# 66 more one-pass products behind the last tile of a two-block transformer kernel, most with interleaved moving columns

## The reference, cut to what matters

```
merged = sum over three branches of sigmoid(G_b) * (branch_b @ w_branch_b)   # 256 x 1024
out    = x + merged @ w_out_2                                                # 256 x 1024
```

## Time and profile before

| | us |
|---|---|
| median of two runs | 974.49 |
| the two runs | 974.24, 974.74 |
| span of the profiled execution, first to last instruction | 970.7 |
| run median less that span | 3.8 |
| TensorE busy in the span | 960.0 |

### The profile page before, as it was taken

How to read it: one execution, slowest core, us unless ns; L and a number is a source line. 1 busy time by engine, 2 the same in 40 slices (tenths; PEclk the granted TensorE clock), 3 DMA queues, 4 the chain that set the end, 5 groups by cost and what they waited for, 6 DMA issues and landing times.

```text
span 970.7 us, 17117 instructions
## 1 busy us (share of the span) xinstructions
PE 960.0 (99%) x7053; PEld 858.6 (88%) x7053; DVE 610.2 (63%) x827; ACT 485.9 (50%) x729; POOL 216.9 (22%) x177
## 2 busy tenths in 40 slices
PE   9999999999999998999999999999999999999998
PEld 8989999999889896899999997778787878999996
DVE  5867554554589899764445447747574646856664
ACT  6446434434364475743443446456545555647452
POOL 0005980000023330000000000414662704920100
PEclk9999999999999999999999999999999999999999
DMA  8764855656554522365565573555455635562461
GB/s 274 221 224 149 275 176 180 196 186 195 190 180 159 175 88 75 126 231 176 186 202 174 186 239 116 198 172 175 142 172 172 190 108 174 176 210 94 136 213 43
DMA packets 119635, 168.73 MB, mean 174 GB/s; under 512 B 5556, under 2 KB 88596, under 8 KB 119572
## 3 DMA queue, kind: packets, MB, share of 16 engines
q1 hardware_dynamic: 119140, 167.66, 53.3%
q10 hardware_dynamic: 432, 0.19, 0.1%
HBM read 165.38 MB, written 2.46 MB: 173 GB/s over the span
## 4 chain that ended last, share of the span: by engine, by line
PE 92%; DVE 4%; ACT 1%; POOL 1%; DMA 1%; issue 1%; SPq 0%; ACTq 0%; DVEq 0%
PE ps L465 26%; PE ps L467 25%; PE ps L466 25%; PE ps L919 2%; PE ps L906 2%; PE ps L892 2%; DVE wlo_sb L445 1%; POOL b_inv_sb L2455 1%; PE ps L553 1%; DMA raw_sb<-w_in_even 1%; PE ps L492 1%; PE ps L566 1%; PE ps L726 1%; PE ps L2077 1%; PE ps L563 1%; PE ps L558 1%
## 5 line engine op out<-in xcount | busy, mean ns | idle before, releaser
L445 DVE TENSOR_TENSOR wlo_sb<-raw_sb,whi_sb 128x2048 fp32r<-128x2048 f32 x143 | 332.7, 2328 | 201.1 <-ACT whi_sb L422 201.1
L422 ACT ACTIVATE whi_sb<-raw_sb 128x2048 fp32r<-128x2048 f32 x143 | 273.9, 1916 | 180.6 <-PE ps L467 163.3
L465 PE MATMUL ps<-hhi_sb,whi_sb 128*128 128x256 f32 x992 | 278.4, 281 | 0.9 <-DVE wlo_sb L445 0.5
L466 PE MATMUL ps<-hlo_sb,whi_sb 128*128 128x256 f32 x992 | 276.9, 279 | 0.0
L467 PE MATMUL ps<-hhi_sb,wlo_sb 128*128 128x256 f32 x992 | 276.8, 279 | 0.0
L465 PEld LDWEIGHTS ps<-hhi_sb,whi_sb 128*128 128x128 f32 x992 | 186.5, 188 | 3.0 <-issue 1.2
L466 PEld LDWEIGHTS ps<-hlo_sb,whi_sb 128*128 128x128 f32 x992 | 186.5, 188 | 0.9
L467 PEld LDWEIGHTS ps<-hhi_sb,wlo_sb 128*128 128x128 f32 x992 | 186.4, 188 | 0.0
L465 PE MATMUL ps<-whi_sb,hhi_sb 128*128 128x512 f32 (+2 forms) x304 | 119.6, 394 | 0.3 <-DVE qkl_sb L2341 0.2
L467 PE MATMUL ps<-whi_sb,hlo_sb 128*128 128x512 f32 (+2 forms) x304 | 116.8, 384 | 0.0
L466 PE MATMUL ps<-wlo_sb,hhi_sb 128*128 128x512 f32 (+2 forms) x304 | 116.7, 384 | 0.0
(11 more groups left out here) (335 smaller groups left out, 1345.8 us busy)
## 6 DMA issues: line engine op xcount, KB each, us to landing
raw_sb<-w_in SPq DMA_DIRECT2D x45, 1024.0 KB, 5.2
raw_sb<-ffn_gate SPq DMA_DIRECT2D x22, 1024.0 KB, 5.3
raw_sb<-ffn_up SPq DMA_DIRECT2D x22, 1024.0 KB, 5.3
raw_sb<-ffn_down SPq DMA_DIRECT2D x22, 1024.0 KB, 5.0
raw_sb<-w_in_even SPq DMA_DIRECT2D x8, 1024.0 KB, 8.4
raw_sb<-w_in_odd SPq DMA_DIRECT2D x8, 1024.0 KB, 5.1
raw_sb<-w_branch SPq DMA_DIRECT2D x6, 1024.0 KB, 5.1
scratch_sb<-bias_rows_dram SPq DMA_DIRECT2D x40, 128.0 KB, 3.0
```

Source lines behind the costliest of these rows:

```text
L422: nc.scalar.activation(place(whi, n0), in_raw(n0), ACT.Copy).then_inc(hi_ready, 1)
L445: nc.vector.tensor_tensor(place(wlo, n0), in_raw(n0), place(whi, n0).bitcast(F32), ALU.subtract).then_inc(lo_ready, 1)
L465: nc.tensor.matmul(dst, l_hi, r_hi, start=first, stop=False)
L466: nc.tensor.matmul(dst, l_hi, r_lo, start=False, stop=False)
```

## The change

Behind the last `mm_rows`, and still in TensorE's program, 66 matmuls follow. They wait for the last three releases of banks 5 to 7 first, then write bank 6. Each stands alone (start and stop).

- 57 of them take `s`, 128 columns of chunk 6 of `hhi`, as stationary operand, and 512 columns of the last `w_out_2` tile in `whi` as moving operand: 19 orders of reading, three products each. `apart(512, d)` reads two streams that are `d` columns apart in turn (for d = 4: columns 0, 4, 1, 5, 2, 6, 3, 7, 8, 12, ...). `streams(512, a, run)` cuts the 512 columns into `a` streams and takes `run` columns of each in turn. The last four are two streams that are 1024, 264, 257 and 256 columns apart, the last of them from column 8 on.
- 9 take 128 columns of the tile as stationary operand and the 256 columns of `hhi`'s chunk 6 as moving one: in order, as two streams 128 apart, and as two such streams taken two columns at a time.

```diff
+            w = place(whi, N_OUT2 + 3)
+            s = hhi[:, 6, 0:P]
+            for k in range(1, 4):
+                pe.wait_ge(*RELEASED[-k])
+
+            def apart(n, d, run=1):
+                return w[:, 0:n].rearrange("p (o a b c) -> p o b a c", a=2, c=run, b=d // run)
+
+            def streams(n, a, run=1):
+                return w[:, 0:n].rearrange("p (a b c) -> p b a c", a=a, c=run)
+
+            forms = [w[:, 0:512]] + [apart(512, d) for d in (256, 128, 64, 32, 16, 8, 4, 2)]
+            forms += [streams(512, a) for a in (4, 8)]
+            forms += [streams(512, a, run) for a, run in ((2, 2), (4, 2), (2, 4), (2, 16))]
+            forms += [w[:, 0:2048].rearrange("p (a b) -> p b a", a=2)[:, 0:256, :],
+                      w[:, 0:528].rearrange("p (a b) -> p b a", a=2)[:, 0:256, :],
+                      w[:, 0:514].rearrange("p (a b) -> p b a", a=2)[:, 0:256, :],
+                      w[:, 8:520].rearrange("p (a b) -> p b a", a=2)]
+            for v in forms:
+                for _ in range(3):
+                    nc.tensor.matmul(ps[:, 6, :], s, v, start=True, stop=True)
+            half = w[:, 0:P]
+            for v in (hhi[:, 6, :], hhi[:, 6, :].rearrange("p (a b) -> p b a", a=2),
+                      hhi[:, 6, :].rearrange("p (a b c) -> p b a c", a=2, c=2)):
+                for _ in range(3):
+                    nc.tensor.matmul(ps[:, 6, 0:T], half, v, start=True, stop=True)
```

## The result

The changed kernel takes 987.75 us, the median of two runs (985.91 and 989.59), against 974.49 before: a ratio of 1.0127, with a 95% interval of 1.0092 to 1.0162. That is 13.3 us more, where 41.3 were forecast. The profiled execution's span is 984.1 us, 13.4 more than in the profile before; its own run took 985.91.

A forecast was written before the change was run, and what follows sets the result against it. TensorE, busy for 99% of the span, was taken to bound the kernel. 44.4 us behind 967.37 plus 0.17 end at 1012.0, 41.3 us of growth; 974.5 + 41.3 = 1015.8 us, range 985 to 1019.

The forecast's parts named there:

- The step that failed: TensorE's moving-operand read: a port fetches 16 bytes in about 1.8 ns; a column outside them costs its own fetch, 0.933 us a product.
- the 1.74 on DVE: DVE addition with elements 64 bytes apart: 1.74 ns an element against 1.062 adjacent, taken to support the fetch price.
- The 4 units: Added 512-column forms that never stay in 16 bytes: four in-order products' time each, 0.933 us; 13 forms, 52 units.
- the four forms counted at 1 unit: Added 512-column forms in order, two apart, and runs of 4 and 16: an in-order product's 0.2333 us each.
- Order is free: Rival at the moving operand's read port: fetches overlap, so order does not matter; 985.7 us, 1.15% more, chance 0.20.
- its variant with the gain: Same free-order case in the added block, 0.017 us less in 54 products and half that in 6: 984.7 us.
- the 3.8 us around the span: Time outside the profiled span, kept unchanged in the sum: 974.5 + 41.3 = 1015.8 us.
- Half pace: Rival for moving-operand reads: far columns cost only twice, limit a two-column word; 995.1 us, or 993.5; chance 0.17.
- distance: Rival for moving-operand reads: memory banks collide at some distances only, half of 13 forms free; 1003.2 us, chance 0.12.
- all dear: Rival in the added block: two apart and runs of 4 and 16 also cost 4 units; 1025.6 us, 0.04 including clock loss.
- The bound below: Lower bound for interleaved products: no cost, or 0.017 us gain if a second stream hides what the first waits for.
- dear reading would lower it: TensorE's clock in the added block: slow reading taken for idleness could drop it to 1.2 GHz, some 2 us more.

The follow-up runs named there:

- e8_lines: Added block replaced by eleven forms of five products pricing a lane's fetch, float32 and 2-byte, against the changed kernel; four 2-byte streams took 0.86 us a product, no run time given.
- e3_outputs: Added block replaced by products varying output order and 2-byte reading, against the changed kernel; 2-byte every eighth column took 0.900 us a product, no run time given.

## Why the prediction was wrong

**What held.** TensorE sets the end and the added work lengthens it; the waits, weight loads and stores cost nothing; the block starts one product behind the last; repeats are not dropped; in order, two apart and runs of 16 go at 0.233 to 0.239 (fours, counted the same, at 0.252); the distance does not matter.

**The step that failed** is the one that began "I take it that a port fetches 16 bytes in about 1.8 ns" and ended in "a column outside the 16 bytes just fetched costs a fetch of its own". The 1.8 ns was right as a price: 1.77 for a lane of float32, 1.76 for 2-byte elements (the 1.74 on DVE rests on a single kind of instruction). But it was right by luck, since it was read off four columns that one port delivers in 1.82 ns. What was wrong is that one port serves all columns and keeps only the 16 bytes just fetched. In one-pass float32, even and odd places have a lane each, so:

- in order, a lane takes two columns of each 16 bytes, so it needs a new 16 bytes for every four places. At 1.77 ns each that is 128 x 1.77 = 0.227 us, above the array's 0.216. That is what holds it, and not a port that gives four columns in 1.82. The measured 0.233 is 0.006 more, and no run says why.
- in two streams, each lane takes four columns one after another and keeps up: 0.216. The 4 units that I gave to 11 forms of 512 columns were 0.92 units.
- 4 and 8 streams cost 1.17 and 2.2 units, not 4; pairs 1.42 and 1.92, not 2. A lane finds one of its last two or three lines again at less than a new fetch.

In the sum: the 33 products of the 11 two-stream forms take 7.12 us in place of 33 x 0.933 = 30.8, which is 23.7 of the 28.6 us that the block was too long by. The four forms with 4 or 8 streams or pairs take 0.82 + 1.54 + 0.99 + 1.34 = 4.7 in place of 8.4, another 3.7; the 256-column forms take 1.3 less, and the four forms counted at 1 unit 0.1 more.

**The rivals.** "Order is free" came nearest: it had less than 2% more and, in its variant with the gain, the right price of the commonest form (0.017 us less); I argued against it that the ordered stream misses the array's pace, which was the reason for the gain. That its 985.7 us is near the profiled run's 985.91 is luck. Its block would have ended at 981.9 us, the measured one ended at 983.9, and the 2.0 us between were made up by the 3.8 us around the span, which are 1.8. Its growth of 11.2 us stands against 13.3. The reason it gave, fetches that overlap for the whole stream, is not what the runs show: eight streams and every second column are dear. "Half pace", distance and "all dear" are out: far columns cost 0.216 us a product at 4 columns apart as at 1024, where these rivals had 0.467 or 0.933 for all such forms or for half of them. The bound below, a gain if a second stream hides what the first waits for, was in the text and should have weighed more: the DVE row is another engine's, and both ends of the price were equally unseen on TensorE.

**A rule of two hits.** A hit is a column taken from the line at hand. Two hits a line absorb the latency, says the Trainium skill (Advanced Engine Details and Errata, SBUF Cachelines). The runs do not agree: in a lane of float32 in order, two hits are not quite enough (0.233 against 0.216), and with 2-byte elements even four are not (0.225). Pairs of columns, which would have been free by that rule, are one hit a visit in each of two lanes and cost 0.332. The measurement decides.

**The base.** The sum stood on a span 2 us below that of the runs in the table, but it was carried as a difference, so nothing was lost by it: the span grew by 13.4 us and the median by 13.3, the latter from two runs 3.7 us apart.

**The clock.** I feared that dear reading would lower it, for 2 us. In the profile after, it stayed at its upper level through 0.513 us products. But where the products of a run were nearly as slow as the forecast had them, it fell twice, with no wait of TensorE ahead: in `e8_lines` at 977.1 us, at the fifth of five products that started 0.86 us apart (0.90, 0.50 and 0.82 in three stretches that follow one another, so at 1.2 GHz for 3.4 us), and in `e3_outputs` at 980.56 us, behind products 0.90 us apart. The other falls on record came during or just behind waits of TensorE of 1.1 to 2.4 us in mid-kernel, or when its last product was done. Whether dear reading brings a fall about is made likely by these two and not shown; no run tried it by itself.

## What to carry to other kernels

A price bounded by another engine's row is a bound and no likeliest value: when the stream at hand misses its own ideal by a little (0.233 against 0.216), ask what structure would make it miss by about that much, since the same structure may make the odd access faster. For one-pass float32 products, read the moving operand as two streams half an operand apart, one column of each in turn, and let the instruction that empties PSUM put the columns back: 7.5% a product, 3.4% of this kernel. Don't do it with 2-byte elements, where it costs 2.2 times, and look for the waits that the faster stream uncovers.

## What the runs showed of the hardware

- One-pass float32 products read even and odd places of the moving operand by a lane each; 2-byte products have one lane. A new 16 bytes costs a lane 1.76 to 1.77 ns (0.453 us for 256 of them, 0.900 for 512).
- Changing among two or three lines that a lane has read lately costs 0.95 to 1.3 ns a change (0.485 / 512 with 2-byte elements, 0.274 / 256 and 0.332 / 256 with float32); with four lines it is 1.7 to 2.0 ns (0.863 / 512, 0.447 / 256, 0.513 / 256). No single rule fitted all of these.
- The output's pairs may lie 256 columns apart in PSUM at no cost (0.233, 0.216), and DVE reads PSUM with every second element at 686 ns for 512, as in order (688), ACT at 600 (601).
- The distance of two streams, from 4 to 1024 columns, and an offset of one column change nothing (0.216 to 0.217).
